# Inverse roots of the norms inside the mixer: sums spread by wide products, roots as logarithm and exponential on ScalarE

## The reference

```python
def rms_norm(x, g):
    return x * lax.rsqrt(jnp.mean(x * x, axis=-1, keepdims=True) + EPS) * g

def hybrid_mixer(h, ...):
    (mq, mkv, mkr, gq, gk, gv, gg, gr, rq, rk, rv, rg) = split(h @ w_in)
    qh  = rms_norm(mq, mla_q_norm_g) @ mla_w_q_up        # latent of 256
    kvh = rms_norm(mkv, mla_kv_norm_g) @ mla_w_kv_up     # latent of 128
    ...                                                  # rotary parts, attention
    o_gla = rms_norm(o_g, gla_norm_g) * silu(gr)         # 4 heads of 64
    o_ret = rms_norm(o_r, ret_norm_g) * silu(rg)         # 4 heads of 64
    return concatenate([o_mla, o_gla, o_ret]) @ w_out
```

## Time and profile before

| | |
|---|---|
| median of 3 runs | 1933.88 us (1932.35 to 1935.47) |
| the profiled execution | 1935.69 us |
| its span, first to last instruction | 1933.9 us |
| busy: PE, DVE, ACT, POOL | 99%, 64%, 41%, 33% of the span |
| mean granted clock of TensorE | 0.996 of full |

### The profile page before, as it was taken

How to read it: one execution, slowest core, us unless ns; L and a number is a source line. 1 busy time by engine, 2 the same in 40 slices (tenths; PEclk the granted TensorE clock), 3 DMA queues, 4 the chain that set the end, 5 groups by cost and what they waited for, 6 DMA issues and landing times.

```text
span 1933.9 us, 31234 instructions
## 1 busy us (share of the span) xinstructions
PE 1908.1 (99%) x12796; PEld 1711.6 (89%) x12796; DVE 1228.1 (64%) x1631; ACT 792.6 (41%) x1148; POOL 643.1 (33%) x490
## 2 busy tenths in 40 slices
PE   8999999999999999999999999999999999999998
PEld 7999988897678999998899999889967789999886
DVE  6888843533555788872578888344355567888523
ACT  5344433334454444442444444233345544444322
POOL 3666500002330566620045664000022325666000
PEclk9999999999999999999999999999999999999999
DMA  4223333321003123333312333332200122322321
GB/s 154 88 109 108 106 122 123 100 102 44 1 23 131 50 104 108 108 109 131 131 44 89 108 109 109 131 130 95 87 23 3 66 87 86 109 96 99 130 99 66
DMA packets 27228, 179.91 MB, mean 93 GB/s; under 512 B 3283, under 2 KB 3445, under 8 KB 7158
## 3 DMA queue, kind: packets, MB, share of 16 engines
q1 hardware_dynamic: 25618, 173.63, 25.1%
q10 hardware_dynamic: 1508, 4.87, 0.8%
HBM read 176.39 MB, written 2.10 MB: 92 GB/s over the span
## 4 chain that ended last, share of the span: by engine, by line
PE 94%; DVE 2%; ACT 2%; issue 1%; POOL 1%; DMA 0%; SPq 0%; POOLq 0%; DVEq 0%; ACTq 0%
PE ps L467 27%; PE ps L469 27%; PE ps L468 27%; PE ps L839 2%; PE ps L857 1%; PE ps L725 1%; PE ps L479 1%; PE ps L646 1%; PE ps L647 1%; PE ps L648 1%; PE ps L734 1%; PE ps L846 1%; PE ps L761 1%; PE ps L781 0%; PE ps L787 0%
## 5 line engine op out<-in xcount | busy, mean ns | idle before, releaser
L467 PE MATMUL ps<-xH,WH 128*128 128x256 f32 (+2 forms) x1408 | 421.3, 299 | 0.9 <-DVE WL L1415 0.8
L469 PE MATMUL ps<-xH,WL 128*128 128x256 f32 (+2 forms) x1408 | 418.7, 297 | 0.0
L468 PE MATMUL ps<-xL,WH 128*128 128x256 f32 (+2 forms) x1408 | 418.7, 297 | 0.0
L467 PE MATMUL ps<-TH,WH 128*128 128x256 f32 x1216 | 344.1, 283 | 0.0
L469 PE MATMUL ps<-TH,WL 128*128 128x256 f32 x1216 | 344.1, 283 | 0.0
L468 PE MATMUL ps<-TL,WH 128*128 128x256 f32 x1216 | 344.1, 283 | 0.0
L1293 DVE TENSOR_TENSOR WL<-raw,WH 128x2048 fp32r<-128x2048 f32 x62 | 143.4, 2313 | 262.3 <-ACT WH L953 249.6
L467 PEld LDWEIGHTS ps<-xH,WH 128*128 128x128 f32 (+1 forms) x1408 | 268.9, 191 | 9.7 <-issue 2.2
L468 PEld LDWEIGHTS ps<-xL,WH 128*128 128x128 f32 (+1 forms) x1408 | 268.8, 191 | 8.4 <-issue 1.0
L469 PEld LDWEIGHTS ps<-xH,WL 128*128 128x128 f32 (+1 forms) x1408 | 268.8, 191 | 7.7
L468 PEld LDWEIGHTS ps<-TL,WH 128*128 128x128 f32 x1216 | 233.5, 192 | 0.0
(11 more groups left out here) (258 smaller groups left out, 3682.0 us busy)
## 6 DMA issues: line engine op xcount, KB each, us to landing
raw<-stream SPq DMA_DIRECT2D x156, 1024.0 KB, 4.8
norm_g<-norm_gains SPq DMA_DIRECT2D x11, 512.0 KB, 5.3
x<-x_in SPq DMA_DIRECT2D x4, 512.0 KB, 7.2
wq<-w_q_up ACTq DMA_DIRECT2D x4, 512.0 KB
out<-x SPq DMA_DIRECT2D x4, 512.0 KB, 2.7
const<-consts ACTq DMA_DIRECT2D x2, 578.5 KB
wkv<-w_kv_up ACTq DMA_DIRECT2D x2, 512.0 KB
cos<-positions ACTq DMA_DIRECT2D x2, 256.0 KB
```

Source lines behind the costliest of these rows:

```text
L467: mm(dst, wh, xh, start=start, stop=False)
L468: mm(dst, wh, xl, start=False, stop=False)
L469: return mm(dst, wl, xh, start=False, stop=stop)
```

## The change

1. The sums of the squares are made by products whose held block is 128x128 of ones (`ones_row`), or of ones within each head of 64 (`same_head`, 128 columns of the constants in place of two), and whose moving side is the whole 128x512 of squares. The sum comes out on every partition at once, so that no spread is needed.
2. ACT makes the inverse root on the whole 128x512: logarithm of sum x scale + EPS from PSUM, then exponential of -0.5 times that, into the tile of the squares. DVE's means and GpSimd's powers go.
3. The steps in the loop: sums in steps 16, 18 and 19, roots on ACT in steps 17 to 20, DVE's multiplications in steps 18 to 21, the high halves in 20 to 23. The squares of the third and fourth tile go to `kf` and `kb`. PSUM banks alternate, so the third sum waits for the first root, and the fourth for the second.
4. The conversion of the second output pair (`high_at(base, 9)`) moves on ACT from step 17 to step 24; its low half on DVE stays at steps 29 and 30.

```diff
-GATE_STEP = NORM_STEP + 5
+GATE_STEP = NORM_STEP + 3
@@ TensorE, projection
                     pe.wait_ge(latent_sq, due(latent_sq, 3))
-                    for c in range(BLK):
-                        tok = slice(c * P, (c + 1) * P)
-                        mm(ps[:, 6, c:c + 1], sq[:, 0, tok], ones[:], start=True, stop=False)
-                        mm(ps[:, 6, c:c + 1], sq[:, 1, tok], ones[:], start=False, stop=True)
-                        last = mm(ps[:, 6, 4 + c:5 + c], acc[:, tok], ones[:], start=True, stop=True)
-                    last.then_inc(col_ready, 1)
+                    mm(ps[:, 6, :], ones_row[:], sq[:, 0, :], start=True, stop=False)
+                    mm(ps[:, 6, :], ones_row[:], sq[:, 1, :], start=False, stop=True).then_inc(latent_summed, 1)
                     pe.wait_ge(in_kept, due(in_kept, 6))
                     values_pair(5, (4, 5))
...
                     last.then_inc(cum_ready, 1)
+                    pe.wait_ge(latent_root, due(latent_root, 1))
+                    mm(ps[:, 6, :], ones_row[:], acc[:], start=True, stop=True).then_inc(latent_summed, 1)
                     pe.wait_ge(in_kept, due(in_kept, 8))
                     pair(6, (0, 1))
                     pe.wait_ge(v_kept, due(v_kept, 2))
-                    pe.wait_ge(rstd_ready, due(rstd_ready, 1))
-                    for c in range(BLK):
-                        tok = slice(c * P, (c + 1) * P)
-                        mm(ps[:, 6, tok], rstd[:, c:c + 1].broadcast_to([P, P]), ident[:], start=True, stop=True)
-                        last = mm(ps[:, 4, tok], rstd[:, 4 + c:5 + c].broadcast_to([P, P]), ident[:], start=True, stop=True)
-                    last.then_inc(spread_ready, 1)
@@ TensorE, loop
-                    def linear_squares(t):
+                    def linear_sums(t):
                         pe.wait_ge(o_sq, due(o_sq, t + 1))
-                        for c in range(BLK):
-                            last = mm(ps[:, LIN_BANKS[0], t * 8 + 2 * c:t * 8 + 2 * c + 2], sq[:, t % 2, c * P:(c + 1) * P],
-                                      head_sel, start=True, stop=True)
-                        last.then_inc(o_sq_used if t < 3 else col_ready, 1)
-                    def linear_spread(t):
-                        if t == 0:
-                            pe.wait_ge(rstd_ready, due(rstd_ready, 2))
                         if t >= 2:
-                            pe.wait_ge(o_normed, due(o_normed, t - 1))
-                        for c in range(BLK):
-                            for h in range(2):
-                                at = t * 8 + 2 * c + h
-                                last = mm(ps[h * DV:(h + 1) * DV, LIN_BANKS[t % 2], c * P:(c + 1) * P],
-                                          rstd[:, at:at + 1].broadcast_to([P, DV]), ident[:], start=True, stop=True)
-                        last.then_inc(o_spread if t < 3 else spread_ready, 1)
+                            pe.wait_ge(o_root, due(o_root, t - 1))
+                        mm(ps[:, LIN_BANKS[t % 2], :], same_head, squares_of[t], start=True, stop=True).then_inc(o_summed, 1)
...
-                        elif NORM_STEP < n <= NORM_STEP + 2:
-                            for t in range(2):
-                                linear_squares(2 * (n - NORM_STEP - 1) + t)
-                        elif GATE_STEP <= n < GATE_STEP + 4:
-                            linear_spread(n - GATE_STEP)
+                        elif n == NORM_STEP + 1:
+                            linear_sums(0)
+                            linear_sums(1)
+                        elif NORM_STEP + 3 <= n < NORM_STEP + 5:
+                            linear_sums(n - NORM_STEP - 1)
@@ ScalarE, projection
+                    def inverse_root(bank, to, scale):
+                        link(af(to, ps[:, bank, :], ACT.Ln, bias=eps_column[:], scale=scale))
+                        return af(to, to, ACT.Exp, scale=-0.5)
                     high_at(base, 5)
                     keep_values(0)
+                    act.wait_ge(latent_summed, due(latent_summed, 1))
+                    inverse_root(6, sq[:, 0, :], 1.0 / QR).then_inc(latent_root, 1)
                     act.wait_ge(z_ready, due(z_ready, 1))
                     link(af(kf[:], ps[:, 7, :], ACT.Abs))
...
                     keep_values(1)
+                    act.wait_ge(latent_summed, due(latent_summed, 2))
+                    inverse_root(6, acc[:], 1.0 / KVR).then_inc(latent_root, 1)
@@ ScalarE, loop
-                                if t >= 2:
-                                    act.wait_ge(o_sq_used, due(o_sq_used, t - 1))
-                                af(sq[:, t % 2, :], heads[:, t, :], ACT.Square).then_inc(o_sq, 1)
-                        elif GATE_STEP + 2 <= n < GATE_STEP + 6:
+                                af(squares_of[t], heads[:, t, :], ACT.Square).then_inc(o_sq, 1)
+                        if NORM_STEP + 2 <= n < NORM_STEP + 6:
+                            t = n - NORM_STEP - 2
+                            act.wait_ge(o_summed, due(o_summed, t + 1))
+                            inverse_root(LIN_BANKS[t % 2], squares_of[t], 1.0 / DV).then_inc(o_root, 1)
+                        if GATE_STEP + 2 <= n < GATE_STEP + 6:
...
-                        if n == NORM_STEP + 2:
+                        if n == NORM_STEP + 9:
                             high_at(base, 9)
@@ VectorE, projection
-                    dve.wait_ge(col_ready, due(col_ready, 1))
-                    ts(mean[:, 0:BLK], ps[:, 6, 0:BLK], 1.0 / QR, EPS, ALU.mult, ALU.add)
-                    ts(mean[:, BLK:2 * BLK], ps[:, 6, BLK:2 * BLK], 1.0 / KVR, EPS, ALU.mult, ALU.add).then_inc(mean_ready, 1)
...
-                    dve.wait_ge(spread_ready, due(spread_ready, 1))
+                    dve.wait_ge(latent_root, due(latent_root, 2))
@@ VectorE, loop: normed_output(t) in steps GATE_STEP to GATE_STEP + 3
+                        dve.wait_ge(o_root, due(o_root, t + 1))
-                        if n in (GATE_STEP + 9, GATE_STEP + 10):
-                            low_half(base, IN_PAIRS + 1, n - GATE_STEP - 9)
+                        if n in (NORM_STEP + 14, NORM_STEP + 15):
+                            low_half(base, IN_PAIRS + 1, n - NORM_STEP - 14)
@@ GpSimd
-                power(0, 8)
-                power(1, 32)
```

More of the change, by code:

```diff
@@ L49 @@
 STAGES = 3 * DEPTH
-NORMS = 2
 SHARES = (0.5, 1.0, 0.5)
@@ L68 @@
 C_HSEL = C_TWICE + 64
-C_INV = C_HSEL + 2
+C_INV = C_HSEL + P
 CONSTS = C_INV + 1
@@ L184, in hybrid_trunk @@
         rstd_x = sb("rstd_x", [P, BLK])
-        mean = sb("mean", [P, 32])
-        rstd = sb("rstd", [P, 32])
+        eps_column = sb("eps_column", [P, 1])
         minus_half = sb("minus_half", [P, 32])
@@ L193, in hybrid_trunk @@
         share = sb("share", [P, 2, BLK])
-        sb("small_end", [P, 40])
+        sb("small_end", [P, 96])
         with ExitStack() as hidden:
@@ L236, in hybrid_trunk @@
         const = sb("const", [P, CONSTS])
-        sb("const_end", [P, 8])
+        sb("const_end", [P, 24])
         zg = sb("zg", [P, SEQ])
@@ L262, in hybrid_trunk @@
         twice = const[:, C_TWICE:C_TWICE + 2 * ROPE]
-        head_sel = const[:, C_HSEL:C_HSEL + 2]
+        same_head = const[:, C_HSEL:C_HSEL + P]
         inv_freq = const[:, C_INV:C_INV + 1]
         pair_out = (kt_gla, kt_ret)
+        squares_of = (sq[:, 0, :], sq[:, 1, :], kf[:], kb[:])
         further = {3: W3, 4: W4, 5: W5}
@@ L309, in hybrid_trunk @@
         xL_ready = sem("xL_ready", 0)
[L310 to L314, removed]
         silu_ready = sem("silu_ready", 0)
@@ L357, in hybrid_trunk @@
         latent_sq = sem("latent_sq", 3)
+        latent_summed = sem("latent_summed", 2)
+        latent_root = sem("latent_root", 2)
         latent_ready = sem("latent_ready", 3)
@@ L382, in hybrid_trunk @@
         o_sq = sem("o_sq", 4)
-        o_sq_used = sem("o_sq_used", 3)
+        o_summed = sem("o_summed", 4)
+        o_root = sem("o_root", 4)
         o_normed = sem("o_normed", 4)
@@ L1279, in _ @@
             nc.vector.memset(ones_row[:], 1.0)
+            nc.vector.memset(eps_column[:], EPS)
             nc.vector.memset(minus_half[:], -0.5).then_inc(start_ready, 1)
@@ L1543, in mixer @@
                     low_at(stage, base, 7)
-                    dve.wait_ge(spread_ready, due(spread_ready, 1))
+                    dve.wait_ge(latent_root, due(latent_root, 2))
                     for j in range(2):
-                        stt(mq[:, j, :], mq[:, j, :], gains_all[:, layer, G_Q + j:G_Q + j + 1], ps[:, 6, :], ALU.mult,
+                        stt(mq[:, j, :], mq[:, j, :], gains_all[:, layer, G_Q + j:G_Q + j + 1], sq[:, 0, :], ALU.mult,
                             ALU.mult).then_inc(latent_ready, 1)
-                    stt(ckv[:], ckv[:], gains_all[:, layer, G_KV:G_KV + 1], ps[:, 4, :], ALU.mult, ALU.mult).then_inc(latent_ready, 1)
+                    stt(ckv[:], ckv[:], gains_all[:, layer, G_KV:G_KV + 1], acc[:], ALU.mult, ALU.mult).then_inc(latent_ready, 1)
```

(18 more changed lines are left out.)

## The result

The changed kernel takes 1944.68 us in the median of five runs (1942.59 to 1952.13), the kernel before 1933.49 beside it (1932.35 to 1935.47). The ratio is 1.0064, 95% interval [1.0054, 1.0075]: slower by more than a measurement can miss. The profiled execution of after took 1942.59 us, the fastest of the five; its span is 1940.8 us.

The account below looks back on a forecast made before the run. PE was taken as the bound, holding 94% of the chain. From 1935.69 us profiled, 2 x (6.5 - 1.8) - 3.05 = +6.4 gave 1942.1; weighing the median's clock, the forecast was 1941.5 us, range 1931 to 1950.

Parts of the forecast that it names:

- What comes to ACT: Inverse roots on ACT: each function brings its own 1.28 us table load, so one root takes 3.88 us.
- Projection: Projection: ACT's extra work is covered by PE without waits, and dropped spread products save 1.8 us per layer.
- Loop: Attention loop: four roots in steps 17 to 20 make PE pause for ACT; +6.5 us per layer.
- The walk: Loop: ACT's work laid end to end from keep_turn(17), so keep_turn(21) ends at 568.5 us and PE waits.
- PE's saving of 4.1 us: Loop: four wide products of 3.44 us replace 7.5 us of sums and spreads, per layer.
- The clock: Layer 0's projection: the clock's fall behind the one-column products goes away; -3.05 us, bounds 0 and -3.05.
- if none had it: Whole kernel: if no run behind the median had the clock's fall, the time is 1933.88 + 9.4 = 1943.3 us.
- Rival 3: In the pauses PE works thinly and the clock falls, one to three times: 1945 to 1953 us; chance 0.11.
- my own: The prediction's main case for the whole kernel: 1937 to 1947 us by itself; chance 0.66.
- Rival 1: Loop, steps 17 to 20: logarithm and exponential share a table, no loads come, faster at 1920.2 us; chance 0.07.
- Rival 2: Loop: pauses shrink to 3 to 4 us per layer, near no change, 1930 to 1937 us; chance 0.14.
- Rival 4: Loop: each of eight table switches per layer costs its load twice, 1.28 us more; 1962 us; chance 0.02.

Follow-up runs that it names:

- e7_one_set: The changed kernel with one table set for logarithm and exponential loaded twice per layer, no loads left in the loop; 1926.11 us, 0.9959 of the kernel before.
- e2: The kernel before with only the loop's part of the change (new norm of the heads, conversion at step 24); 1947.4 us, ratio 1.0069.
- e4: The changed kernel with the third and fourth sum one step later; 1946.51 us, 1.0066 of the kernel before.
- e5: The changed kernel with the conversion of the second output pair back at step 17; 1949.84 us, 1.0089 of the kernel before.
- e1b_latents: The kernel before with only the projection's part (new norm of the latents), large tiles at their old addresses; 1930.43 us, ratio 0.9993.
- e11_last_psum: e7_one_set with ACT writing each layer's fourth root to its PSUM bank instead of SBUF; 1925.1 us, 0.9948 of the kernel before.
- e8_shift32: The kernel before with only 32 bytes more padding in SBUF, shifting the large tiles behind it; 1939.29 us, 1.0030 of the kernel before.

## Why the prediction was right, and where its sum was off

**What comes to ACT: right.** Eight loads per layer in the loop, one more in the projection, a root 3.92 us against 3.88. Walked end to end from keep_turn(17), keep_turn(21) was to end 21.0 us later; it ended 21.2 later, with no idle time between. The two kernels without loads show that this is the cause.

**Projection: right.** The logarithm of the gate was done at 436.6 (437.2 worked out), PE came to its cumulative sums at 441.5 (441.9), the second root was ready at 445.9 (446.3), and PE waited for none of them. (Each is some 0.5 us early because the whole kernel was, 377.06 against 377.59 at the last transposes.) The half by itself gave -1.88 in an undisturbed mixer against -1.8.

**Loop: right in the sum, less so in its terms.** +6.41 in both layers against +6.5. But the pauses were 9.57 us and not 11.5, as values(20) waited 0.50 instead of 2.3: the clock had fallen to 0.50 at 552 us and PE was itself late there. The fourth sum held PE for 1.72 us, where the same one in e7_one_set, at full clock, held it for 0.87. The walk held the clock at full. It came out all the same, because ACT's list sets when the stretch ends: what PE loses to the low clock it waits less. PE's saving of 4.1 us was a little too large. In e7_one_set the pauses from step 17 to values(25) are 3.02 us against 1.17 before, and the loop is 1.77 shorter, so that PE's work shrank by 3.6. By distances of starts the old sums and spreads took 7.42 us (7.5 in the sum) and the four new sums 3.59 (3.44).

**The clock: the term that was mis-sized.** "I take -3.05" took one execution's fall for that of most. The fall was in the profiled execution, and gone from it after the change as forecast (windows at 432 and 436 us, 1.00). But on one chip 12 of 15 executions of the kernel before had a mean clock of 0.997 or more and took 1932.98 to 1934.17 us, and three had 0.996 and took 1934.78 to 1935.82. So the median had nothing to give back, and the case "if none had it" was the true one: 1943.3, measured 1944.68, against the 1941.5 that was forecast. The mixers' own part is 2 x (6.41 - 1.88) = 9.1 us of the 11.2 by the medians. The other 2.1 would be about one fall like that at 1370 us; where the median execution had its falls is not known, as only the fastest has a trace.

**Rival 3 came on top, but not by its mechanism alone.** Falls do go with the pauses: in the traces of the four kernels with eight loads (after, e2, e4, e5) all eight loops have one, in those of the six with fewer or none 2 loops of 12. But PE's pauses also take up most of what such a fall costs: after's loops have one each and differ by 0.01 us, and only longer ones (e2_heads layer 0, e4_sums_later layer 1) added 1.6. It costs time where PE does not wait, 1.67 us in e1b_latents and 1.48 in after's second projection, where no pause lies ahead of it. The five runs go with their mean clocks: 0.997, 0.995, 0.995, 0.992, 0.990 with 1942.59, 1943.85, 1944.68, 1948.39 and 1952.13 us. I gave this 0.11 as a case by itself; it is a spread on top of my own.

**Rival 1 fell as stated, and can be had.** The loads come, so the kernel as written does not have it. With the set loaded by hand it does: 1926.1, not 1920.2. Of the 5.9 us between, 3.05 is the clock's term just told. The rest is in the loop, which got 1.77 us shorter per layer in the profile of e7_one_set where 3.5 (4.1 less 0.6) were counted: the pauses grew by 1.85 us instead of 0.6, and PE's work shrank by 3.6 instead of 4.1. DVE's slow multiplication is 1.1 us of the pauses, which e11_last_psum shows. The Trainium skill's rule (ScalarE: Activation LUTs, "Table sets: the hidden batching unit"), that one load serves a logarithm and an exponential, holds on this chip once that set is the one in place (e7_one_set, no load between 541.95 and 543.19), and did not describe what the kernel got by itself.

**Rival 2 fell:** +6.41 per layer. **Rival 4 fell:** one function starts 0.01 us behind its load, and the eight loads lengthen the loop by 9.26 us against e11_last_psum, 1.16 each, where the rival needed 2.56. The drain of 1.38 us in the Trainium skill (ScalarE: Activation LUTs, "What ACT_TABLE_LOAD costs") does not show in any row here.

## What to carry to other kernels

Count the table loads that a function brings, two for each logarithm and exponential pair here, before moving work to ScalarE, and look whether one set that holds both can be put in place once: it turned +0.6% into -0.4%. Lay a busy engine's list end to end through the steps; where it has no idle time, moving the waits about (other banks, later sums) only changes their name. And don't credit a profiled execution's clock to the median of the runs: look first how often it falls.

## What the runs showed of the hardware that was not expected

VectorE's product of two fp32 128x512 operands took 1.86 us instead of 0.75 beside a busy GpSimd when both came from SBUF, and 0.75 when one came from PSUM (e7_one_set and e11_last_psum, both layers). The Trainium skill (SBUF — State Buffer, "Who interferes with whom") says that an instruction of VectorE with two SBUF inputs contends with one of GpSimd that reads SBUF; the trace agrees. The change had moved this operand from PSUM to SBUF, and the prediction priced it at nothing. In the change as written that was right: all four multiplications took 0.75 us in after, in both layers, since GpSimd was idle beside them or began in their last 0.2 us. The price came when the loads were gone and the work moved closer together.

Moving the tiles that lie behind one small pad by 32 bytes cost 0.3% with no other edit: the 128x512 products of the SwiGLU stages went from 390 to 396 ns, and a stage from 349.28 to 350.22 us (e8_shift32). Why the address matters was not looked into.
